# Moving the first token tile ahead of the weight pieces in the combination with values

## The reference, cut to what matters

```python
out = ... y.reshape(p, d).astype(jnp.float32) * w_buf[:, None]   # two experts per token, weighted
xc = xc + cg2 * out[:n_ctx].reshape(xc.shape)                    # context tokens
x = x + g2 * out[n_ctx:].reshape(x.shape)                        # latent tokens
...
h_ctx = modulate(rmsnorm(xc, norm_g[i, 0]), csh1, csc1)
h_lat = modulate(rmsnorm(x, norm_g[i, 0]), sh1, sc1)
z = h @ w_in            # columns of v and gate are computed in this stage
```

## Time and profile before

| | us |
|---|---|
| median of 3 runs | 3095.43 |
| lowest, highest run | 3095.36, 3097.83 |
| profiled execution | 3097.77 |
| its span from first to last instruction | 3096.0 |

### The profile page before, as it was taken

How to read it: one execution, slowest core, us unless ns; L and a number is a source line. 1 busy time by engine, 2 the same in 40 slices (tenths; PEclk the granted TensorE clock), 3 DMA queues, 4 the chain that set the end, 5 groups by cost and what they waited for, 6 DMA issues and landing times. The chain is left out here.

```text
span 3096.0 us, 40551 instructions
## 1 busy us (share of the span) xinstructions
PE 2522.7 (81%) x13249; PEld 2036.0 (66%) x13249; DVE 2031.6 (66%) x2005; ACT 1398.7 (45%) x1452; POOL 358.7 (12%) x401
## 2 busy tenths in 40 slices
PE   4488872695799999999939989968694899999970
PEld 0466662584688888888827867756584688888860
DVE  1569999666657777588435303358565788888855
ACT  0311001451546667577434313334331677777752
POOL 0000000100100010011012110055100111001104
PEclk8589886796799999999969999989896899999995
DMA  9344341321878899799555311024551999999956
GB/s 305 117 164 154 129 155 55 112 103 50 323 261 308 319 333 339 267 383 388 225 194 185 116 56 34 8 96 145 193 197 41 367 389 384 386 388 396 394 220 227
DMA packets 294339, 689.12 MB, mean 223 GB/s; under 512 B 22764, under 2 KB 49588, under 8 KB 294222
## 3 DMA queue, kind: packets, MB, share of 16 engines
q1 hardware_dynamic: 263058, 584.81, 52.4%
q0 software_dynamic: 17472, 56.72, 5.5%
q10 hardware_dynamic: 13712, 46.30, 4.0%
HBM read 597.74 MB, written 91.06 MB: 222 GB/s over the span
## 5 line engine op out<-in xcount | busy, mean ns | idle before, releaser
L1479 DVE TENSOR_TENSOR moe_w_lo<-moe_w_raw,moe_w_hi 128x2048 fp32r<-128x2048 f32 x384 | 861.9, 2286 | 81.4 <-ACT moe_w_hi L1408 45.6
L1408 ACT ACTIVATE moe_w_hi<-moe_w_raw 128x2048 fp32r<-128x2048 f32 x384 | 713.8, 1908 | 60.1 <-issue 38.2
L99 PE MATMUL moe_pg<-moe_w_hi,moe_xt_hi 128*128 128x512 f32 x592 | 243.3, 411 | 11.6 <-DVE moe_xt_lo L1490 5.9
L99 PE MATMUL moe_py<-moe_w_hi,moe_at_hi 128*128 128x512 f32 x592 | 241.5, 408 | 11.8 <-DVE moe_w_lo L1479 8.2
L100 PE MATMUL moe_pg<-moe_w_lo,moe_xt_hi 128*128 128x512 f32 x592 | 236.4, 399 | 0.0
L101 PE MATMUL moe_pg<-moe_w_hi,moe_xt_lo 128*128 128x512 f32 x592 | 236.1, 399 | 0.0
L100 PE MATMUL moe_py<-moe_w_lo,moe_at_hi 128*128 128x512 f32 x592 | 234.9, 397 | 0.0
L101 PE MATMUL moe_py<-moe_w_hi,moe_at_lo 128*128 128x512 f32 x592 | 234.7, 396 | 0.0
L101 PE MATMUL moe_pu<-moe_w_hi,moe_xt_lo 128*128 128x512 f32 x592 | 234.3, 396 | 0.0
L99 PE MATMUL moe_pu<-moe_w_hi,moe_xt_hi 128*128 128x512 f32 x592 | 234.1, 396 | 0.0
L100 PE MATMUL moe_pu<-moe_w_lo,moe_xt_hi 128*128 128x512 f32 x592 | 234.1, 396 | 0.0
(11 more groups left out here) (348 smaller groups left out, 5419.5 us busy)
## 6 DMA issues: line engine op xcount, KB each, us to landing
moe_w_raw<-in_moe_w SPq DMA_DIRECT2D x384, 1024.0 KB, 12.4
taps_ada_w<-in_ada_w SPq DMA_DIRECT2D x40, 1024.0 KB, 6.9
scratch_experts_out<-moe_y ACTq DMA_DIRECT2D x57, 512.0 KB, 6.4
taps_raw<-in_conv_pw_w SPq DMA_DIRECT2D x20, 512.0 KB, 8.7
scan_v<-scratch_gla_values SPq DMA_DIRECT2D x20, 512.0 KB, 3.6
ada_w<-in_ada_w SPq DMA_DIRECT2D x4, 2048.0 KB, 30.3
cv_raw<-in_gla_w_in SPq DMA_DIRECT2D x16, 512.0 KB, 4.6
scratch_gla_out<-scan_o SPq DMA_DIRECT2D x16, 512.0 KB, 6.5
```

The lines of the kernel that those rows point to most:

```text
L99: pe.matmul(out, xh, wh, start=start, stop=False)
L1408: act.activation(hi[m][:, cut, :], raw[m][p][:, cut, :], ACT.Copy).then_inc(s(f"{m}_hi{h}"), 1)
L1479: dve.tensor_tensor(lo[m][:, cut, :], raw[m][p][:, cut, :], hi[m][:, cut, :].bitcast(F32), ALU.subtract).then_inc(s(f"{m}_lo{h}"), 1)
```

## The change

Three hand-written orders change; no instruction is added or taken away in this stage.

```diff
 # SyncE's queue
                 load_x(0)
                 for q in range(RB):
                     load_w(q)
+                for q in range(RB, PIECES):
+                    load_w(q)
                 load_x(1)
-                for q in range(RB, 2 * PIECES):
+                for q in range(PIECES, PIECES + RB):
                     load_w(q)
                 for t in range(TILES):
                     store_x(t)
                     if t + 2 < TILES:
                         load_x(t + 2)
+                    if t == 0:
+                        for q in range(PIECES + RB, 2 * PIECES):
+                            load_w(q)
...
 # ScalarE
-                for q in range(PIECES):
+                first(0)
+                for q in range(2):
                     w_high(q)
-                first(0)
-                for t in range(TILES + 1):
+                root(0)
+                for q in range(2, PIECES):
+                    w_high(q)
+                scale(0)
+                first(1)
+                high(0)
+                for t in range(1, TILES + 1):
                     if t + 1 < TILES:
                         first(t + 1)
-                    if t < 2:
-                        w_high(PIECES + 2 * t)
-                        w_high(PIECES + 2 * t + 1)
+                    if t < 3:
+                        w_high(PIECES + 2 * (t - 1))
+                        w_high(PIECES + 2 * (t - 1) + 1)
...
-                    if t >= 1:
+                    if t >= 2:
                         high(t - 1)
...
 # VectorE
-                for q in range(PIECES):
+                second(0)
+                for q in range(2):
+                    w_low(q)
+                rstd(0)
+                for q in range(2, PIECES):
                     w_low(q)
                 dve.wait_ge(s("cols_ready"), 2)
-                for t in range(TILES + 1):
+                modulate(0)
+                low(0)
+                for t in range(1, TILES + 1):
                     if t < TILES:
                         second(t)
-                    if t < 2:
-                        w_low(PIECES + 2 * t)
-                        w_low(PIECES + 2 * t + 1)
-                    if t >= 1:
+                    if t < 3:
+                        w_low(PIECES + 2 * (t - 1))
+                        w_low(PIECES + 2 * (t - 1) + 1)
+                    if t >= 2:
                         modulate(t - 1)
                     if t < TILES:
                         rstd(t)
-                    if t >= 1:
+                    if t >= 2:
                         low(t - 1)
```

## The result

The changed kernel takes 3104.00 us (median of 19 runs, 3097.59 to 3107.19), the kernel before 3096.01 us (19 runs, 3093.65 to 3100.21). The ratio is 1.0024 with a 95% interval of 1.0017 to 1.0031: **the change costs 5 to 10 us** (8.0 by the medians), where I had forecast +0.8 us and a range up to 3100.5. The profiled execution of the changed kernel has a span of 3100.5 us.

A forecast was written before the change was run, and what follows sets the result against it. The start of `product(V0,1)` on TensorE was taken to set the stage's end; tile 0's 10.0 us gain vanishes in the wait for the latent row, leaving +0.8 us on the median 3095.43: 3096.2 us, range 3091.2 to 3100.5.

The forecast's parts named there:

- What bounds the stage: TensorE: from the start of `product(V0,1)` it runs through, so the stage's end stands at a fixed distance from that instant.
- Tile 0 comes forward, 10.0 us: Start of tile 0's product on TensorE: `product(V0,0)` at 1609.6 instead of 1619.64, with piece 3 landing in 3.5 us.
- New work ahead of tile 1's chain: VectorE: `second(2)` and pieces 6 and 7 now precede `modulate(1)`; the latent row is issued at 1617.3, against 1614.06.
- The term that decides, the landing of the row: Latent row of `cv_gate` on SyncE's queue: lands 7.1 us after issue, at 1624.4; ends 3.5 and 8.8 us.
- The sum: Start of `product(V0,1)`: 1634.4 against 1633.58, +0.8 us; with the ends of the row's landing -2.8 and +2.5 us.
- The pause of TensorE: TensorE between the transposes of tile 1 and `product(V0,1)`: idle for 15.9 us.
- The clock: TensorE's clock at the two products: both again start at the lower level, so it adds no term.
- rival 3: Slower: the row lands late, every us more is lost; at 13.6 us +7.3 us, 3102.7; chance 0.07 beyond +2.5.
- Rival 1: The row is in time and piece 7 holds tile 1's chain: -5.8 us, 3089.6; chance 0.07.
- Rival 2: The whole gain arrives: `modulate(1)` runs once tile 1 is transposed, `product(V0,1)` moves by 10.0 us, 3085.4; chance 0.04.

## Why the prediction was wrong, step by step

*What bounds the stage*: right. In all kernels whose TensorE has no later wait for data, the next stage's first matmul comes 218.6 to 219.4 us behind `product(V0,1)`; most of that spread is the time of the product itself.

*Tile 0 comes forward, 10.0 us*: it was 8.3. The mis-sized term is the landing of piece 3, taken as the shortest of the trace, 3.5 us. The tile view of cv_raw for its issue alone says

```profile
DMA to landing us min/median/max: 5.6/5.6/5.6
```

against my 3.5; it went out 0.3 us earlier than I had reckoned, so 1.8 us of the 2.1 arrive. My reason, queues nearly empty at that moment, did not hold: piece 2 was issued only 1.1 us ahead of it, two gathers of tile 2 shortly before, and the DMA engines were 57% busy from 1592 to 1594 and 77% from 1594 to 1596. In the other profiles it took 4.7 to 6.2 us. What costs how much of that stays open, only residual tile 1 right behind it is ruled out. Since this term lies on the way to the row as well, it cost 1.8 us there.

*New work ahead of tile 1's chain*: right, and the order of the waits too. The row was issued at stage time 40.7, my sum says 38.3: 1.8 us from piece 3, and 0.8 from SyncE's queue, which took 2.19 us from piece 7 to the row, not 1.41; the load of residual tile 3 took 1.14 us to issue. 0.2 us less from the small rest.

*The term that decides, the landing of the row*: this is **the step that failed**. I took 7.1 us, with 8.8 as the upper end; it was 10.9, and 11.0 in the second profile of the same kernel. Two numbers behind that upper end were wrong. I counted seven transfers. GpSimd's issues in the changed kernel are

```profile
1613.30 1.02 POOL L1849 DMA_INDIRECT cv_y<-scratch_experts_out,plan_slot  x1 [0.30 <-issue]
1617.30 0.95 POOL L1849 DMA_INDIRECT cv_y<-scratch_experts_out,plan_slot  x1 [2.97 <-DVE cv_mix L2022]
1618.55 0.94 POOL L1849 DMA_INDIRECT cv_y<-scratch_experts_out,plan_slot  x1 [0.30 <-issue]
```

three, and another of 1611.12 was still under way: the DMA view from 1613 to 1630 us

```profile
DMA packets 1552, 4.72 MB, mean 278 GB/s; under 512 B 144, under 2 KB 144, under 8 KB 1552
```

holds nine times 512 KB. And I let them all move at the 393 GB/s of the earlier trace rows. Busy time by stretch (columns as in the earlier trace rows) says

```profile
1616.00:1622.00 6.00, 2.19 (x14) 1.46 (x12) 1.03 (x1) 3.13 (x3) 1.89 (x2) 0.84 0.93 279
1622.00:1628.00 6.00, 0.00 (x0) 0.00 (x0) 0.00 (x0) 1.06 (x1) 0.00 (x0) 0.50 0.99 404
```

279 GB/s while the DMA engines were 93% busy, and 404 only afterwards. Nine transfers in the 13.8 us from about 1614.2 to 1628 are 342 GB/s; my seven at 393 were 9.3 us. By an estimate from these figures 2.7 us of the difference come from the two transfers more (nine at 393 are 12.0 us) and 1.8 us from the rate. That pieces with their rows of 2 KB move more slowly than the residual tiles is a guess that no run here tests.

The Trainium skill's rule (DMA: Bandwidth & Descriptors, section Queues, rings and completion order), that a queue starts its descriptors in order and that the DMA engines take turns between queues, was the better guide. This case agrees with both parts, though it does not single them out: in SyncE's queue pieces 6 and 7, the store and the row landed in the order of their issue, at 1620.9, 1622.6, 1624.7 and 1628.9, and transfers of either queue cost the row time, 2.8 us for the pieces ahead of it and 2.9 us for the gathers in the other queue. I had cited it for 8.8 us and still chose the row of before.

*The sum*: with the measured issue (+2.4) and landing (+3.8) in the place of mine, +0.8 becomes +7.0; the chain behind the row took 9.75 us, not 9.95, which leaves the measured +6.7, but for rounding. *The pause of TensorE*: 20.45 us instead of 15.9, for the same reason.

*The clock*: two starts at the lower level, as expected (the first matmuls take 0.80 us), but the second was dearer: `product(V0,1)` took 8.11 us to the next transposes, 7.70 before. Of these 0.4 us 0.3 arrive: the next stage starts 7.0 and not 6.7 us later.

*The rivals*: rival 3, the late row, is what happened, with the mechanism and the price of a us for a us that I had given it; its chance of 0.07 was the mistake, since the 13.6 us beside it were evidence that a tile behind three others can take that long. The measured +6.7 is also close to the +7.3 of that rival, but by luck: it had a landing of 13.6 us from an issue 2.4 us earlier. Rival 1's floor, piece 7 at a sum of -5.8, was -2.3 in the run without the row (52.3 against 54.6): piece 7 went out 1.4 us later than I had reckoned, mostly piece 3 again, and landed in 6.7 us, not 4.6. Rival 2 did not come, and no version reached its 10 us: the best had `product(V0,1)` 9.3 us earlier, once VectorE's order was changed as well.

## What to carry to other kernels

When a chain is moved ahead, write down for each engine what now stands between the moved part and the next thing that the bound engine wants, and follow every transfer in that list to its place in its queue: here a row of 512 KB, needed once, went behind four others in its queue and took back more than the whole gain. Size a landing by all that is under way beside it, in every queue, at the rate of a stretch with the same mixture; the row of the kernel before is no price for a moved transfer. The gain was there to be had: with the row issued first and the pieces that nobody needs yet put last, the kernel is 0.2 to 0.3% faster than before.

## What the runs showed of the hardware that I had not expected

A product of 24 matmuls, begun at the lower clock after a pause, does not always take the same time. `product(V0,0)`, which all the edits leave alone, took 7.38 us from its start to the next transposes in the changed kernel and 8.22 us in the run with the pieces behind the row. `product(V0,1)` took 7.70 us before, 8.11 and 7.82 in the two profiles of the changed kernel, and up to 8.47 us (the run with residual tile 1 late, 1629.72 to 1638.19). With such a product on the path two executions can differ by 0.3 to 0.8 us.

One and the same transfer of 512 KB, the latent row, took 4.1 to 4.3 us where it met a short backlog, 8.0 us where the DMA engines were moving 420 GB/s when it was issued, and 10.9 us in the changed kernel. The issue of residual tile 3 by SyncE grew from 0.33 us before to 1.14 us in that crowd.
